# A causal-mean mixer moved from VectorE's channel-major adds to a TensorE product over tokens

## The reference, cut to what matters

```
sh, sc, g = mods[3], mods[4], mods[5]          # rows of silu(c) @ ada_w + ada_b, 1024 each
h = rms_norm(x, norm_g) * (1 + sc) + sh        # 256 tokens x 1024 channels
for gi, w in enumerate((2, 4, 8, 16)):         # 256 channels each
    pooled[gi] = (sum of the last w tokens of h) / min(t + 1, w) - h
y = einsum('btgc,gcd->btgd', pooled, w_pool)   # 256x256 a group
x = x + (1 + g) * (y * pool_scale)
```

## Time and profile before

| what | us |
|---|---|
| median of 3 runs | 1470.73 |
| profiled execution, whole | 1470.9 |
| its span | 1469.1 |
| TensorE busy | 1400.5 |
| VectorE busy | 959.9 |
| ScalarE busy | 666.1 |

### The profile page before, as it was taken

How to read it: one execution, slowest core, us unless ns; L and a number is a source line. 1 busy time by engine, 2 the same in 40 slices (tenths; PEclk the granted TensorE clock), 3 DMA queues, 4 the chain that set the end, 5 groups by cost and what they waited for, 6 DMA issues and landing times.

```text
span 1469.1 us, 16759 instructions
## 1 busy us (share of the span) xinstructions
PE 1400.5 (95%) x6801; PEld 1140.1 (78%) x6801; DVE 959.9 (65%) x1086; ACT 666.1 (45%) x870; POOL 22.5 (2%) x44
## 2 busy tenths in 40 slices
PE   7999998899999999998799999999999996999998
PEld 6986556788888888886688888877888884788887
DVE  3448875866667876667877667666667758554544
ACT  4445544544444634345533435453343545544342
POOL 2200000000000000000000000000000000000000
PEclk8998898999999999999899999999999998999999
DMA  8878525657777588884288784547778631265551
GB/s 240 220 256 245 187 86 193 243 189 275 279 288 257 183 305 280 288 284 163 84 301 294 278 289 156 172 172 257 257 267 286 220 123 50 86 201 180 192 185 73
DMA packets 164993, 315.45 MB, mean 215 GB/s; under 512 B 6955, under 2 KB 114789, under 8 KB 155701
## 3 DMA queue, kind: packets, MB, share of 16 engines
q1 hardware_dynamic: 161872, 305.54, 60.8%
q0 software_dynamic: 2864, 8.80, 2.2%
q10 hardware_dynamic: 180, 0.05, 0.0%
HBM read 312.00 MB, written 1.84 MB: 214 GB/s over the span
## 4 chain that ended last, share of the span: by engine, by line
PE 85%; DVE 9%; ACT 3%; issue 2%; DMA 1%; SPq 0%; ACTq 0%; DVEq 0%
PE bank L667 25%; PE bank L669 25%; PE bank L668 25%; PE bank L759 2%; PE bank L687 2%; DVE full L1634 1%; DMA raw<-in_w_in 1%; PE bank L967 1%; PE bank L690 1%; DVE acc L1558 1%; PE bank L714 1%; ACT whi L1201 1%; DVE wlo L1571 1%; PE bank L958 1%; PE bank L950 1%
## 5 line engine op out<-in xcount | busy, mean ns | idle before, releaser
L1571 DVE TENSOR_TENSOR wlo<-raw,whi 128x2048 fp32r<-128x2048 f32 x205 | 469.2, 2290 | 282.2 <-ACT whi L1201 281.8
L1201 ACT ACTIVATE whi<-raw 128x2048 fp32r<-128x2048 f32 x205 | 392.1, 1913 | 206.5 <-PE bank L669 200.1
L667 PE MATMUL bank<-whi,uhi 128*128 128x512 f32 (+2 forms) x1088 | 431.1, 396 | 12.1 <-DVE mix L1885 3.7
L669 PE MATMUL bank<-whi,ulo 128*128 128x512 f32 (+2 forms) x1088 | 421.5, 387 | 0.0
L668 PE MATMUL bank<-wlo,uhi 128*128 128x512 f32 (+2 forms) x1088 | 420.8, 387 | 0.0
L667 PEld LDWEIGHTS bank<-whi,uhi 128*128 128x128 f32 x1088 | 207.3, 190 | 58.3 <-issue 12.0
L669 PEld LDWEIGHTS bank<-whi,ulo 128*128 128x128 f32 x1088 | 206.8, 190 | 42.4
L668 PEld LDWEIGHTS bank<-wlo,uhi 128*128 128x128 f32 x1088 | 207.2, 190 | 40.1 <-issue 1.2
L667 PE MATMUL bank<-whi,hsplit 128*128 128x512 f32 (+1 forms) x512 | 201.8, 394 | 2.0 <-DVE hsplit L1711 2.0
L669 PE MATMUL bank<-whi,hsplit 128*128 128x512 f32 (+1 forms) x512 | 199.6, 390 | 0.0
L668 PE MATMUL bank<-wlo,hsplit 128*128 128x512 f32 (+1 forms) x512 | 199.5, 390 | 0.0
(11 more groups left out here) (238 smaller groups left out, 1129.2 us busy)
## 6 DMA issues: line engine op xcount, KB each, us to landing
raw<-in_ffn_w_in SPq DMA_DIRECT2D x176, 512.0 KB, 4.8
ada<-in_ada_w SPq DMA_DIRECT2D x72, 1024.0 KB, 7.1
raw<-in_ffn_w_out SPq DMA_DIRECT2D x44, 1024.0 KB, 5.1
raw<-in_w_in SPq DMA_DIRECT2D x16, 1024.0 KB, 8.5
raw<-in_w_mlp_in SPq DMA_DIRECT2D x16, 1024.0 KB, 6.6
raw<-in_w_mlp_out SPq DMA_DIRECT2D x16, 1024.0 KB, 5.0
ada<-in_kv_ada_w SPq DMA_DIRECT2D x8, 1024.0 KB, 7.3
raw<-in_w_kv SPq DMA_DIRECT2D x8, 1024.0 KB, 5.2
```

The source lines that it names most:

```text
L667: nc.tensor.matmul(o, sh, mh, start=start, stop=False, skip_group_check=skip)
L669: return nc.tensor.matmul(o, sl, mh, start=False, stop=stop, skip_group_check=skip)
L1201: ins = nc.scalar.activation(whi[:, ring(n), :], raw[:, ring(n), :], ACT.Copy)
L1571: ins = nc.vector.tensor_tensor(wlo[:, ring(n), :], raw[:, ring(n), :], whi[:, ring(n), :].bitcast(F32), ALU.subtract)
```

## The change

- The scale (times the norm's gain) and the shift of the pool layer come as rows, `crow[4]` and `crow[3]`, so that they can be applied before any transposition, token by token.
- h is formed token-major in `wide_t` by two VectorE operations a half. A matmul with h as the stationary operand and a constant banded matrix (256 x 256, minus the identity, 1088 columns in four groups) gives pooled directly, channel-major, in PSUM. `windows_across` adds what the first 128 tokens give to the next 15.
- The two halves of the tokens run one behind the other: `pooled(0)`, then `windows(1, ...)`, then `pooled(1)`.
- The pieces of mods 3 and 4 become halves (4 matmuls of 512 columns), and pieces are moved: 3's second half to slot 3 of mlp, 6 and 7 into ffn0, 17's second half into ffn1, the rest spread over the turns of pool and ffn1.
- 38 `keep_busy` transposes of the pool stage go; the turn of ffn1 has 8 in place of 14. GpSimd loads four more rows or tables.

```diff
-for _where, _pieces in (... ((1, 1), ((3, None, 7, 16), (2, 0, 4, 0), (2, 1, 5, 0))),
-                        ((2, 0), ((4, None, 7, 0), (6, None, 7, 8), (7, None, 7, 16))),
+                        ((1, 1), ((2, 0, 4, 0), (2, 1, 5, 0), (3, 0, 6, 0))),
+                        (("mlp", 3), ((3, 1, 7, 0),)),
+                        ((2, 0), ((4, 0, 6, 0), (4, 1, 7, 0))),
                         ((2, 1), ((5, 0, 4, 0), (5, 1, 5, 0))),
-                        ((3, 1), ((18, None, 7, 0), (19, None, 7, 8), (8, 0, 4, 0), (8, 1, 5, 0))),
-                        ((4, 0), ((17, 0, 4, 0), (17, 1, 5, 0))),
+                        (("ffn0", 3), ((6, None, 7, 0),)),
+                        (("ffn0", 5), ((7, None, 7, 0),)),
+                        ((3, 0), ((18, None, 7, 0),)),
+                        ((3, 1), ((19, None, 7, 8), (8, 0, 4, 0))),
+                        ((4, 0), ((8, 1, 5, 0),)),
+                        ((4, 1), ((17, 0, 6, 0),)),
+                        (("ffn1", 3), ((17, 1, 7, 0),)),
...
+            ada_row("c3", 3, 3)
             pool.wait_ge(x_ready, 4)
             ada_row("c5", 1, 5)
+            ada_row("c4", 4, 4)
+            pool.dma_start(pool_g, A["norm_g_2"][0, 1].partition_broadcast(P)).then_inc(pool_in, 16)
+            pool.dma_start(band, band_dram).then_inc(pool_in, 16)
...
-                if e in (4, 5, 7):
+                if e == 4:
+                    pe.wait_ge(x_ready, 16)
+                    keep_busy(8, bank[3])
+                if e in (5, 7):
...
+            def windows(t, c):                                       # TensorE
+                pe.wait_ge(pool_h, 2 * t + c + 1)
+                for k in range(4):
+                    kk = 4 * c + k
+                    h = wide_t[:, t, kk * P:(kk + 1) * P]
+                    ins = nc.tensor.matmul(bank[2 * t + c][:, k * P:(k + 1) * P], h,
+                                           band[:, kk // 2, 144:272] if t else band[:, kk // 2, 0:P],
+                                           start=t == 0, stop=True, skip_group_check=True)
+                ins.then_inc(u_turned, 1)
+            def windows_across():
+                pe.wait_ge(x_ready, 12)
+                for kk in range(KT):
+                    nc.tensor.matmul(bank[2 + kk // 4][:, kk % 4 * P:kk % 4 * P + 16], wide_t[:, 0, kk * P:(kk + 1) * P],
+                                     band[:, kk // 2, P:144], start=kk % 4 == 0, stop=False, skip_group_check=True)
+            def pooled(t):                                           # 2 x 12 matmuls of 256 columns
+                for c in range(2):
+                    pe.wait_ge(u_lo, 12 + 2 * t + c + 1)
...
             n = START["pool"]
-            turn_u(3, 0)
-            keep_busy(14, bank[6])
-            turn_u(3, 1)
-            window(3, 1)
-            pe.wait_ge(pool_full, 3)
-            keep_busy(24, bank[6])
-            pe.wait_ge(lo_done, n + 1)
+            pe.wait_ge(pool_in, 32)
+            windows(0, 0)
+            windows(0, 1)
+            window(3, 0)
+            windows_across()
+            pe.wait_ge(lo_done, n + 1)
+            pooled(0)
+            windows(1, 0)
+            windows(1, 1)
+            window(3, 1)
+            pooled(1)
...
             conv(n + 1)                                              # ScalarE
-            norm(3, 0)
-            norm(3, 1)
+            for t in range(2):
+                for c in range(2):
+                    act.wait_ge(x_ready, 8 + 2 * t + c + 1)
+                    link(square(half_of(xt, t, c), half_of(mix_t, t, c), t, c))
+                root(t, 0).then_inc(pool_root, 1)
+            for t in range(2):
+                for c in range(2):
+                    act.wait_ge(u_turned, 12 + 2 * t + c + 1)
+                    nc.scalar.activation(uhi[:, 4 * c:4 * c + 4, t * P:(t + 1) * P],
+                                         bank[2 * t + c][:].rearrange("p (k n) -> p k n", k=4), ACT.Copy).then_inc(u_hi, 1)
+                if t == 0:
+                    conv(n + 2)
...
-                    m = PIECES[r][2]                                 # VectorE, take_sums
+                    m, half = PIECES[r][2:4]
+                    if m == 4:
+                        dve.wait_ge(pool_in, 32)
+                        c = slice(512 * half, 512 * half + 512)
+                        link(nc.vector.tensor_tensor(crow[4][:, c], crow[4][:, c], pool_g[:, c], ALU.mult))
...
+            def pool_input(t):                                       # VectorE
+                dve.wait_ge(pool_root, t + 1)
+                for c in range(2):
+                    s = slice(512 * c, 512 * c + 512)
+                    link(nc.vector.scalar_tensor_tensor(out=wide_t[:, t, s], in0=xt[:, t, s], scalar=st[:, t, 3:4],
+                                                        in1=crow[4][:, s], op0=ALU.mult, op1=ALU.mult))
+                    nc.vector.tensor_tensor(wide_t[:, t, s], wide_t[:, t, s], crow[3][:, s], ALU.add).then_inc(pool_h, 1)
+            def pool_low(t):       # for c: wait u_hi; ulo = bank[2 * t + c] - uhi, 128 x 512
...
+            add_half(3, 0)
             conv(n + 1)
+            add_half(3, 1)
+            pool_input(0)
+            pool_low(0)
+            pool_input(1)
+            add_half(4, 0)
+            pool_low(1)
+            add_half(4, 1)
+            make_full(4, 0, scal[:, SA["ffn1"], :], mods[:, 6, :])
+            u_low(4, 0)
+            conv(n + 2)
+            make_full(4, 1, scal[:, SA["ffn1"], :], mods[:, 6, :])
+            u_low(4, 1)
             take_window(3)
```

More of the change, by code:

```diff
@@ L140 @@
 _at = 0
-for _n, _w in (("ident", 128), ("ones", 128), ("swap", 128), ("causal", 256), ("cmpmask", 32), ("poolrc", 64),
+for _n, _w in (("ident", 128), ("ones", 128), ("swap", 128), ("causal", 256), ("cmpmask", 32),
                ("cos", 256), ("sin", 256)):
@@ L171, in shape_constants @@
     put("cmpmask", m)
-    rc = np.stack([1.0 / np.minimum(np.arange(16) + 1, w) for w in (2, 4, 8, 16)]).astype(np.float32)
-    put("poolrc", np.broadcast_to(rc[None], (P, 4, 16)))
+    band = []
+    tok = np.arange(T)
+    for w in (2, 4, 8, 16):
+        ago = tok[None] - tok[:, None]
+        m = np.where((ago >= 0) & (ago < w), 1.0 / np.minimum(tok[None] + 1, w), 0.0) - np.eye(T)
+        band.append(np.concatenate([m[:P, :P], m[:P, P:P + 16], m[P:, P:]], 1))
+    band = np.concatenate(band, 1).astype(np.float32)
     dist = 255 - np.arange(384)
@@ L183, in shape_constants @@
     mask[8:] = np.where((dist < 0) | (dist >= 128), NEG, 0.0)
-    return c, onehot, mask
+    return c, onehot, mask, band
 NAMES = ["x", "norm_mix_pre", "norm_mix_post", "norm_mlp_pre", "norm_mlp_post", "w_in", "cmp_pos_k", "cmp_w1_k",
@@ L191, with build @@
          "q_norm_2", "w_o_2"]
-def build(nc, A, cst_dram, onehot_dram, dmask_dram, bias_dram, out):
+def build(nc, A, cst_dram, onehot_dram, dmask_dram, band_dram, bias_dram, out):
     with ExitStack() as ctx:
@@ L237, in build @@
         ident, ones = const("ident"), const("ones")
-        SA = {"ffn0": 0, "pool": 1, "ffn1": 2, "kv": 3, "ffn2": 4, "moba": 5, "ffn3": 6}
+        SA = {"ffn0": 0, "ffn1": 2, "kv": 3, "ffn2": 4, "moba": 5, "ffn3": 6}
         QSC = 7
@@ L290, in hb @@
             return hsplit[:, (p % 2) * 1024:(p % 2) * 1024 + 512], hsplit[:, (p % 2) * 1024 + 512:(p % 2) * 1024 + 1024]
-        pool_a = cols(wide, 0, KT, 272)
-        pool_b = cols(arena, 0, KT, 272)
+        crow += [arena[:, 0:D], arena[:, D:2 * D]]
+        band = cols(arena, 2048, 4, 272)
+        pool_g = arena[:, 3136:3136 + D]
         k2 = cols(wide, 0, KT, T)
@@ L476, in f_bank, with turned @@
             return bank[(4 if v == 7 else 0) + 2 * t + c]
+        def turned(e):
+            return e - (e > 3)
         def wait_f(eng, v, t, c):
@@ L701, in window @@
                 for r in WINDOW.get((v, part), ()):
-                    if r and r == WINDOW.get((v, 0), WINDOW[v, part])[0]:
+                    if v != 4 and r and r == WINDOW.get((v, 0), WINDOW[v, part])[0]:
                         pe.wait_ge(mods_done, r)
@@ new lines, in windows_across @@
+            def windows_across():
[6 more added lines that the diff above has]
+                    pe.wait_ge(u_lo, 12 + 2 * t + c + 1)
+                    for g in (2 * c, 2 * c + 1):
+                        for k in range(2):
+                            ins = mm3(bank[2 * t + c][:, (g % 2) * T:(g % 2 + 1) * T], uhi[:, 2 * g + k, tokens(t)],
+                                      ulo[:, 2 * g + k, tokens(t)], v8(whi, n)[:, 2 * g + k, :],
+                                      v8(wlo, n)[:, 2 * g + k, :], k == 0, k == 1)
+                    ins.then_inc(pe_done if t and c else f_ready, 1)
@@ L1579, in norm_g @@
                 return vec[:, a:a + 8]
-            GAIN_OF = {1: ("ffn0", norm_g(0, 0)), 4: ("pool", norm_g(0, 1)), 7: ("ffn1", norm_g(0, 2)),
+            GAIN_OF = {1: ("ffn0", norm_g(0, 0)), 7: ("ffn1", norm_g(0, 2)),
```

(15 more changed lines are left out.)

36 lines of the change are left out of this document (9 added, 27 removed), and 1 row of the table pair.

## The result

The changed kernel took 1461.68 us (median of 5 runs, 1458.42 to 1464.80) against 1470.55 of the kernel before (5 runs). The ratio on record is 0.9918, 95% interval 0.9901 to 0.9935: 0.8% faster, where 0.3% had been forecast. The two medians alone give 0.9940, 8.9 us less, so the size of the gain in whole executions is known to some 3 us only; the kernel before took 1474.04 at the median of 17 runs and 1475.25 of 19 in later batches. The profiled execution took 1458.97 us, its span 1457.2, 11.9 less than the span of the one profiled execution before.

A forecast was written before the change was run, and what follows sets the result against it. TensorE was taken as the bound, busy 95% of the span. Pool stage -7.3, streams +5.5, turn before mlp -3.0, turn before ffn0 +0.3 sum to -4.5 us: 1466.2 us by the median, 8 in 10 within 1459.0 to 1474.5.

The forecast's parts named there:

- the turn ahead of mlp: Row and one-column pieces between transposes and mlp's first matmul become L690 x6: 3.0 us gained, bounds 1.4 to 4.3.
- the likeliest case: Whole kernel: the summed forecast of 1466.2 us, own range 1463.0 to 1469.5, chance 0.48.
- all cases: Whole kernel, likeliest case and rivals together: 8 in 10 lie in 1459.0 to 1474.5 us.
- the term for the pool stage: ffn0's last matmul to ffn1's first: half clock well into `pooled(0)`, ffn1 starting at 713.3 against 720.57, gain 7.3 us.
- Turns that I had left at nothing: Behind the pool stage, turns of keys and values, queries and to the end: forecast difference 0.
- the streams cost what they carry: Pieces moved into mlp, ffn0 and ffn1 have no cover there: 0.9 + 2 x 1.84 + 0.9 = 5.5 us lost.
- the turn ahead of ffn0: Transposes wait for ScalarE's scaling, 0.9 us left gained; VectorE's longer list loses 1.3: net 0.3 lost.
- `conv(n + 3)` was hidden: In ffn1, `take_window` delays `conv(n + 3)` by 1.1 us against slack of about 1.3: taken as 0, bounds 0 and 1.
- full clock throughout: Rival, pool stage: the clock holds despite the 5.2 us gap, gain 13.3 in place of 7.3, total 1460.2; chance 0.20.
- VectorE as the bound: Rival, new turns before ffn0, in ffn1 and pool stage: VectorE's serial list adds stalls, 3.7 us more, total 1469.9; chance 0.18.
- transposes that nobody reads: Pool stage before the change: 24 filler transposes, 4.52 us, counted in the 39.9 us between ffn0 and ffn1.

The follow-up runs named there:

- The run that came 1.25 us later: The kernel with the sums in the gap plus 11 unread transposes (1.25 us) in mid-ffn1: 1166.8 us from the first transposes ahead of mlp.
- the kernel with the sums in the gap: Changed kernel, pool stage's sums over partitions (mods 18, 19, half of 8) moved into TensorE's gap ahead of the banded products: ratio 0.9895.

## Why the prediction was wrong

The direction and most of the mechanism held, the size didn't: -4.5 forecast, -11.9 between the profiled executions, -12.1 by the ratio, -8.9 by the medians alone. The median, 1461.68, lies below the range of the likeliest case (1463.0 to 1469.5) and within that over all cases. Of the 7.4 us missed between the traces 3.9 lie in the pool stage, 1.2 in the turn ahead of mlp, and the rest in later turns.

- *The failed step* is the term for the pool stage, "I take half clock until `pooled(0)` has run for about as long as the 24 transposes did". That gave 14 us at half without a break. The clock was half twice for short: under the first banded products, and under the first 15 matmuls of `pooled(0)`. In between it was full, so L708 and L1140 took 1.84 and 2.05 instead of 3.2 each, and `pooled(0)` took 4.4 instead of 5.0. From the start of L708 to the end of `pooled(0)` that makes 7.95 us where the sum had 11.4: 3.4 of the 3.9 us between the measured 29.1 and my 33.0 in the same measure (713.3 less 680.33). I had priced the banded products right (3.65 at half against 3.6 forecast) but had not counted them as work under which the clock comes back, although it had come back under 24 transposes. The trace before showed the same once more in this very stage, and I had overlooked it: half clock under the four row pieces (L690, from 690.12 on), and full again by 693.5, before it fell once more in the long wait.

```profile
691.00:693.00 2.00, 2.00 (x4) 0.67 (x2) 0.05 (x1) 0.32 (x1) 0.00 (x0) 0.50 0.24 67
694.00:698.00 4.00, 0.00 (x0) 0.00 (x0) 3.89 (x6) 0.00 (x0) 0.00 (x0) 0.87 0.45 159
```

  All other steps of the stage came as forecast: the gap 5.04 (5.2), pieces 19 and 8 together 2.7 (2.8), the first matmul of ffn1 3.3 behind `add_half(4, 1)` (3.4).
- *The turn ahead of mlp*: 4.2 gained where I took 3.0 out of 1.4 to 4.3. The run with piece 3 alone moved shows the cause, a clock that returns sooner (at 290.4 us there and at 290.6 in the changed kernel, against 297.6 before).
- *Turns that I had left at nothing*: -2.8, +1.4 and -1.0 behind the pool stage. The run that came 1.25 us later switched the first two back from the lengths of the kernel with the sums in the gap (9.7 and 7.0) to those of the changed kernel (6.9 and 8.6). I had treated a later stage as if a shift could not change its length. For the last one there is no such run; the clock was half for 10.2 us before (from 1226.0) and for 6.8 after (from 1215.6) there.
- *Right*: the streams cost what they carry (+5.0 in ffn0 with VectorE's late list at 1.24, +0.9 in ffn1); the turn ahead of ffn0 waits for ScalarE, and what it gained made up for the piece in mlp (+0.1 together); `conv(n + 3)` was hidden. The prediction's own working for that turn was off by little: 1.6 less (3.6 - 3.12) is 1.1 and not 0.9, and 0.9 gained with 1.3 lost is 0.4 lost and not 0.3.
- *Rivals*: full clock throughout (1460.2) gave the nearest total, but by luck, since its stage would have been 27.0 and not 29.1, and the turns made up for it. VectorE as the bound held at one place only, the one that the sum had already. What I had called "transposes that nobody reads" as if free for the taking was worth nothing net.

Shown by runs: the prices in streams, the effect of piece 3, of the gap, of the pieces' place, of pipelining, of VectorE's list, and, in one execution, of a shift. Open: how the pool stage's gain divides between the banded products and the moved pieces; the 1.0 us at the end; and why the clock held in the turn ahead of ffn0 when the product with the gain came later, seen in one profile.

## What to carry to other kernels

A busy engine is not yet an engine at full clock: look up both. One-column sums on the path cost their length here and, in the turn ahead of mlp, the clock as well (5.0 us for a piece of 3.2); the same sort of sums in a gap that waits for another engine cost neither. So ask of each turn whether it has such a gap. Piece 3 had none, and moving it into a gapless stream gained 3.5 us. Pieces 6 and 7 lay ahead of a wait for ScalarE; moving them into a stream cost 1.9, and moving 6 back (with half of mod 4 into mlp) gained 2.1. Judge a change of under 1% by distances within a trace from the last mark that both kernels share, and expect later turns to move by up to 3 us each by a shift alone.

## What the runs showed of the hardware that was not expected

- A plain f32 matmul is two instructions in the trace. At full clock 16 such instructions took 1.84 us with one column, 1.88 with 16 columns and 1.95 with 128: about 0.12 us each, whatever the columns. In the stretch 690.50 to 693.00 the weight loads were busy for all of its 2.50 us, so they may set this pace; no run tests that.
- The clock can be half while TensorE is busy: under L687 in 288 to 294 it was 0.50 with TensorE busy 6.00 of 6.00 us. Transposes in f32 held and raised it: 40 of them kept 1.00 over the gap, and in the kernel before it rose from 0.50 to 1.00 while only the 24 had run.
- In all twelve profiles the clock fell 0.1 to 0.4 us behind the first transposes of the turn ahead of mlp, though these came at 286.8 to 292.3 us. In the two profiles of the changed kernel the distances behind them agreed to 0.1 us, while totals spread by 6.
